# Hybrid HGRN2 and differential-attention block: the adaLN weights arrive in two halves instead of three parts

## The reference, cut to what matters

```python
mod = silu(c) @ w_ada + b_ada                       # 1024 x 3072 weights
shift, scale, gate = split(mod, 3)
h = rms_norm(x, g_pre) * (1 + scale) + shift
proj = h @ w_in                                     # 1024 x 6144
o_a = hgrn2(proj...)  ;  o_b = diff_attention(proj...)
y = (sigmoid(ma) * (o_a @ w_a) + sigmoid(mb) * (o_b @ w_b)) @ w_out
x = x + gate * rms_norm(y, g_post)
```

## Time and profile before

| | |
|---|---|
| median of 3 runs | 928.02 us (925.66 to 929.46) |
| profiled execution | 927.85 us |
| its span | 926.1 us |
| TensorE busy | 855.8 us (92%) |
| VectorE busy | 569.2 us (61%) |
| ScalarE busy | 444.2 us (48%) |
| GpSimd busy | 445.4 us (48%) |
| granted TensorE clock, mean | 0.984 of full |

### The profile page before, as it was taken

How to read it: one execution, slowest core, us unless ns; L and a number is a source line. 1 busy time by engine, 2 the same in 40 slices (tenths; PEclk the granted TensorE clock), 3 DMA queues, 4 the chain that set the end, 5 groups by cost and what they waited for, 6 DMA issues and landing times. The chain is left out here.

```text
span 926.1 us, 12964 instructions
## 1 busy us (share of the span) xinstructions
PE 855.8 (92%) x4825; PEld 673.5 (73%) x4825; DVE 569.2 (61%) x691; ACT 444.2 (48%) x808; POOL 445.4 (48%) x348
## 2 busy tenths in 40 slices
PE   0898799999999999999999999898999999999996
PEld 0786577777777677777777777676788778778885
DVE  3887875688794977776887858545410522892322
ACT  5776322686444865436864436765433710321111
POOL 6042565355455445553554555456778654740000
PEclk9999999999999999999999999999999999999998
DMA  9911341102102110121021021011221732111232
GB/s 330 312 43 50 114 114 46 30 18 69 47 4 66 46 57 13 47 69 31 16 69 47 1 69 46 16 54 46 68 78 37 268 131 80 34 57 46 91 107 75
DMA packets 74481, 68.10 MB, mean 74 GB/s; under 512 B 3700, under 2 KB 65204, under 8 KB 74420
## 3 DMA queue, kind: packets, MB, share of 16 engines
q1 hardware_dynamic: 74304, 67.25, 22.5%
q10 hardware_dynamic: 116, 0.03, 0.0%
HBM read 58.88 MB, written 8.39 MB: 73 GB/s over the span
## 5 line engine op out<-in xcount | busy, mean ns | idle before, releaser
L596 POOL TENSOR_TENSOR w_lo<-w_raw,w_hi 128x512 fp32r<-128x512 f32 x140 | 190.2, 1360 | 279.9 <-ACT w_hi L1145 278.0
L878 PE MATMUL pj<-b_hi,w_hi 128*128 128x512 f32 x616 | 264.6, 430 | 15.0 <-DVE dk L1473 6.5
L880 PE MATMUL pj<-b_hi,w_lo 128*128 128x512 f32 x616 | 243.6, 395 | 0.0
L879 PE MATMUL pj<-b_lo,w_hi 128*128 128x512 f32 x616 | 243.0, 395 | 0.0
L878 PEld LDWEIGHTS pj<-b_hi,w_hi 128*128 128x128 f32 x616 | 117.2, 190 | 54.2 <-issue 9.3
L880 PEld LDWEIGHTS pj<-b_hi,w_lo 128*128 128x128 f32 x616 | 116.9, 190 | 26.3
L879 PEld LDWEIGHTS pj<-b_lo,w_hi 128*128 128x128 f32 x616 | 117.3, 190 | 23.1 <-issue 4.1
L1145 ACT ACTIVATE w_hi<-w_raw 128x512 fp32r<-128x512 f32 x132 | 82.5, 628 | 65.5 <-PE pj L880 58.4
L577 POOL TENSOR_TENSOR w_raw<-w_raw,w_raw 128x512 f32<-128x512 f32 x66 | 93.2, 1412 | 2.9
L1160 ACT ACTIVATE p<-sp,cols 128x1024 f32<-128x1024 f32 (+7 forms) x64 | 46.8, 737 | 0.7
L1298 ACT ACTIVATE y_hi<-y 128x1024 fp32r<-128x1024 f32 x8 | 8.5, 1061 | 76.6 <-DVE y L1669 76.6
(11 more groups left out here) (250 smaller groups left out, 1690.8 us busy)
## 6 DMA issues: line engine op xcount, KB each, us to landing
w_raw<-in_w_in SPq DMA_DIRECT2D x96, 256.0 KB, 4.2
x_in<-in_x SPq DMA_DIRECT2D x8, 512.0 KB, 7.3
ada<-in_w_ada SPq DMA_DIRECT2D x16, 256.0 KB, 7.0
ada<-in_w_ada SPq DMA_DIRECT2D x8, 512.0 KB, 7.1
ada_g<-in_w_ada SPq DMA_DIRECT2D x8, 512.0 KB, 4.6
wo_raw<-in_w_out SPq DMA_DIRECT2D x8, 512.0 KB, 4.2
res<-in_x SPq DMA_DIRECT2D x8, 512.0 KB, 4.3
out_x<-y2n SPq DMA_DIRECT2D x8, 512.0 KB, 2.9
```

The source lines that it names most:

```text
L596: pool.tensor_tensor(w_lo[slot(v)][:, :], raw[:, :], w_hi[slot(v)][:, :].bitcast(F32), ALU.subtract).then_inc(s_wlo, 1)
L878: pe.matmul(bank[:, :], wh, part(b_hi[m], kk), start=(fresh and kk == 0), stop=False, skip_group_check=True)
L879: pe.matmul(bank[:, :], wh, part(b_lo[m], kk), start=False, stop=False, skip_group_check=True)
L880: last = pe.matmul(bank[:, :], wl, part(b_hi[m], kk), start=False, stop=(kk == 3), skip_group_check=True)
```

## The change

The pieces become (0, 4) and (4, 8), each of eight transfers of 512 KB. Tiles 4 to 7 of the second piece lie over tiles 0 to 3 of the first, and SP waits for the first four sums ahead of them. `mod_columns` is done twice instead of three times, with 8 logical products each time: before the first group and after the fourth. On ScalarE `blocks(2, 4)` follows the scaling of x tiles 6 and 7 without a wait. On VectorE the sums of the second piece are interleaved with `block_low(0)` to `block_low(4)`.

```diff
--- before.py
+++ after.py
@@ -118,7 +118,7 @@
 GATEA_AT, MULA_AT = (25, 28), (26, 29)
 GATEA_0, MULA_0 = (30, 33), (31, 34)
 EVICT_AT = {19: (2, 0), 23: (2, 1), 27: (3, 0), 29: (3, 1)}
-PIECES = [(0, 2), (2, 4), (4, 8)]
+PIECES = [(0, 4), (4, 8)]
 
 
 def units(m):
@@ -209,8 +209,7 @@
         b_hi = [block_at(f"b_hi{m}", 4 * m, 2, F32R) for m in range(PROD)]
         b_lo = [block_at(f"b_lo{m}", 4 * m + 2, 2, F32R) for m in range(PROD)]
         b_raw = [block_at(f"b_raw{m}", 4 * m + 2, 2) for m in range(PROD)]
-        ADA_AT = [[8 + kk / 2 for kk in range(KT)], [12 + kk / 2 for kk in range(KT)],
-                  [4 + kk for kk in range(KT)]]
+        ADA_AT = [[8 + kk for kk in range(KT)], [4 + kk for kk in range(KT)]]
         ada = [[block_at(f"ada{p}_{kk}", ADA_AT[p][kk], (b - a) / 4) for kk in range(KT)]
                for p, (a, b) in enumerate(PIECES)]
         acc = block_at("acc", 36, 2)
@@ -482,10 +481,10 @@
                 load_half(half, 0)
             for p, (a, b) in enumerate(PIECES):
                 for kk in range(KT):
-                    if p == 2 and kk == 0:
-                        sp_.wait_ge(s_acc, KT)
+                    if p == 1 and kk == 4:
+                        sp_.wait_ge(s_acc, 4)
                     sp_.dma_start(ada[p][kk][:, :].rearrange("p (z f) -> p z f", z=2),
-                                  w_mod[kk * P:(kk + 1) * P, :, a * P:b * P]).then_inc(s_ada[p % 2][kk // 2], 16)
+                                  w_mod[kk * P:(kk + 1) * P, :, a * P:b * P]).then_inc(s_ada[p][kk // 2], 16)
             for half in range(2):
                 load_half(half, 1)
             for n, t in enumerate((lambda_q1, lambda_k1, lambda_q2, lambda_k2)):
@@ -825,12 +824,10 @@
                     if kk == 0:
                         pe.wait_ge(s_wlo, j + 1)
                     first_product(j, 0, 0, kk)
-                if kk == 0:
-                    mod_columns(1)
-                elif kk < 3:
+                if 0 < kk < 3:
                     for n in range(4):
                         x_block(KT + 4 * (kk - 1) + n)
-            mod_columns(2)
+            mod_columns(1)
             pe.wait_ge(s_xt, 2 * KT)
             for j in range(4):
                 if j == 3:
@@ -1022,7 +1019,6 @@
             blocks(0, 2)
             scale_x(6)
             scale_x(7)
-            act.wait_ge(s_mod, 2)
             blocks(2, 4)
             for n in range(KT, KT + 4):
                 x_out(n)
@@ -1030,7 +1026,7 @@
             for n in range(KT + 4, 2 * KT):
                 x_out(n)
             blocks(5, 8)
-            act.wait_ge(s_mod, 3)
+            act.wait_ge(s_mod, 2)
             blocks(8, 16)
             act.wait_ge(s_lamd, 1)
             act.activation(lam_exp, lam_sum, ACT.Exp).then_inc(s_lame, 1)
@@ -1342,7 +1338,7 @@
                 a, b = PIECES[p]
                 part_acc = acc[:, 2 * P * a:2 * P * b]
                 if kk % 2 == 0:
-                    dve.wait_ge(s_ada[p % 2][kk // 2], 64 if p == 2 else 32)
+                    dve.wait_ge(s_ada[p][kk // 2], 32)
                 if kk == 0:
                     dve.tensor_scalar(part_acc, ada[p][kk][:, :], c_silu[:, 0:1], None, ALU.mult).then_inc(s_acc, 1)
                 else:
@@ -1376,30 +1372,21 @@
             norm(1)
             for kk in range(KT):
                 add_ada(0, kk)
+            mod_piece(0)
             add_ada(1, 0)
+            block_low(0)
             add_ada(1, 1)
-            mod_piece(0)
+            block_low(1)
             add_ada(1, 2)
+            block_low(2)
             add_ada(1, 3)
-            block_low(0)
+            block_low(3)
             add_ada(1, 4)
             add_ada(1, 5)
-            block_low(1)
+            block_low(4)
             add_ada(1, 6)
             add_ada(1, 7)
-            add_ada(2, 0)
             mod_piece(1)
-            add_ada(2, 1)
-            block_low(2)
-            add_ada(2, 2)
-            block_low(3)
-            add_ada(2, 3)
-            add_ada(2, 4)
-            add_ada(2, 5)
-            block_low(4)
-            add_ada(2, 6)
-            add_ada(2, 7)
-            mod_piece(2)
             for e in range(5, 8):
                 block_low(e)
             for kk in range(4):
```

## The result

The changed kernel takes 931.56 us in the median of 13 runs (928.66 to 934.83), the kernel before 926.96 in the median of 13 (925.66 to 930.74). The ratio is 1.0045, interval 1.003 to 1.006: 4.2 us slower (0.0045 x 927), where +4.9 was forecast and 932.9 named. The two medians differ by 4.6 us. By the ratio it lies just inside the 0.5% that the forecast took as its bound, on the side of "no change" (chance 0.42), though the interval excludes 1.000. The profiled execution took 930.91, its span is 929.1.

A forecast was written before the change was run, and what follows sets the result against it. TensorE was taken as busiest, its first product held by a chain of sums, columns and first block. Terms 3.9 + 2.4 - 0.3 - 0.8 - 0.3 = +4.9 us on the median 928.02 gave 932.9, range 929.6 to 935.6.

The forecast's parts named there:

- Part 1: VectorE's first sum, grown from 512 to 1024 columns per tile, ends at 32.50 against 28.59: +3.9 us.
- Part 2: TensorE's first columns take 16 passes instead of 8, mostly at half clock, 3.4 us: +2.4 us.
- Rival (a): Clock stays up through TensorE's first columns, 16 passes at 1.95 us: +3.5 us in all, 931.5; chance 0.26.
- Part 3: From first columns to first product: ScalarE's start follows in 0.43 us instead of 0.70, -0.3 us; the 2.88 behind stay.
- Part 4: Second columns leave TensorE's product stream, -0.8 us; last columns no longer held by the sums, -0.3 us.
- Part 5: ScalarE's 4.03 us wait for the second part goes, without gain; later scaling of x tiles 6 and 7 is hidden.
- rival (d): ScalarE's 4.0 us of waiting sets the stream, so its removal pays back nearly all: 928.9; chance 0.04.
- Part 6: SP waits for four sums instead of eight; modulation weights and `w_raw` loads come earlier; cost and gain 0.
- Rival (b): Half clock lasts longer in TensorE's products, up to +1.2, sum +6.6, 934.6, chance 0.12; if shorter by half, -0.9.
- Rival (c): TensorE's idle times before 82.18 and 112.78 swallow the delay: 928, no change; chance 0.05.

The follow-up runs named there:

- e1_loads: The kernel before with only its transfers in the two halves of the change, sums and columns still in three parts: 928.74 us, ratio 1.0014 to the kernel before.
- e3_warm_after: The changed kernel with 40 identity transposes ahead of the first columns and 28 behind them, to keep the clock up: 929.86 us, ratio 1.0023 to the kernel before.
- second profile: Profile of a repeat of the unaltered changed kernel, on the same chip as its variants: 932.72 us, ratio 1.0046 to the kernel before.
- e4_columns: The kernel before with its first columns computed three times, 24 passes in place of 8: 929.85 us, ratio 1.0026 to the kernel before.

## Why the prediction was right, step by step

- **Part 1 (sums, +3.9)**: measured 10.2 - 6.2 = +4.0. Right. It is read from the traces; no run changes the sums alone. The cover of the transfers was some 1.6 us by e1_loads, 1.4 in the forecast.
- **Part 2 (columns, 3.4 us)**: measured 3.54 in both profiles, near the upper bound. The clock is at half from the start of the columns; e3_warm_after takes it away and gets 1.84. In the first profile it fell only as the columns began, so that the full 3.5 us there was a near thing. Rival (a), the clock stays up, did not occur in a profile of the changed kernel. Two profiles don't exclude it in other executions.
- **Part 3**: from the columns' end (36.47) to ScalarE 0.44, and 39.78 - 36.91 = 2.87 from there, forecast 0.43 and 2.88. First product forecast at 39.3, measured 39.8, of which 0.2 is the later first sum.
- **Part 4**: first product to last columns 55.99 - 39.78 = 16.2, forecast 16.3; the sums ended at 54.2, before TensorE arrived. In the second profile it is 17.1, by the longer half clock.
- **Part 5**: no wait in the stream for the third `b_lo` or for x. ScalarE's 4.03 us of waiting went, 6.13 ahead of the first block took its place, and TensorE gained nothing by the first: rival (d) fails.
- **Part 6**: right. SP issued the four `w_raw` loads from 29.35 instead of 32.83, and GpSimd still waited for TensorE, until 61.28 instead of 57.75.
- **Rival (b)**, a half-clock stretch of differing length, is real but small: twelve products took 4.38 and 5.26 us in two executions of the same kernel. Its sum for a stretch half as long is slightly off: 3.3 us halved saves 0.8, not 0.9.
- **Rival (c)**, swallowing: at 118.39 the profile is 5.6 us late, and e4_columns excludes that all is swallowed. The pause ahead of that place has more in it than the forecast saw: VectorE waits there 3.85 us before and 3.95 after for the gate's weights. But SP issues these transfers when VectorE's `b_lo` is done (106.89 and 112.41), so they move with the work. The sentence that everything behind the last `mod_piece` moves with it was too strong: the forecast put at nothing what VectorE pays beside GpSimd, and this took 1.1 us off the delay at the lambda multiply and put 1.1 on again at 107.48.
- The **size** was 0.7 too large against the ratio (4.2), 0.3 against the medians (4.6), well inside the interval of 2.8 to 5.6. What makes up the 0.7 was not separated; one execution's meetings with GpSimd and half-clock stretches move it by 1.1 to 1.6 us each. That the profiled pair shows 4.1 at 217 us, close to the ratio's 4.2, is chance: it was 5.6 at 118 us, and 2.9 at 542.

Not tried: sums of the first half alone in the changed order (with transfers in three parts), since a sum over four feature blocks needs both parts' data.

## What to carry to other kernels

Where the first use of a result waits for a chain (load, reduce, convert), the size of the first piece sets the start, and merging pieces to have fewer instructions pays the saved time where nothing waits and the added time where all does. Price the first piece alone, from the trace's row of the larger form. When an edit lengthens a pause of TensorE, look at the granted clock of the work right behind it: here 1.7 of the 6.5 us by which the first product is later are the clock's, and with 16 short transposes in the pause the kernel before measured about 0.14% faster, which one of two intervals does not tell from no change. Follow a delay over several marks: here it was 5.2, 4.0, 5.6 and 4.1 us on the way, and any one of them alone would have misled.

## What the runs showed of the hardware

- The clock did not come back during 3.54 us of one-column passes without a gap: in the changed kernel the first products, behind the passes and a pause of 3.30 us, still ran at 1.2 GHz (40.34 and 40.77, 0.43 us apart). With sixteen transposes directly behind full-clock work in the kernel before it stayed at 2.4 GHz over the 1.76 us of pause that followed them and through the products, where without them the products started at 1.2 GHz.
- Executions of one kernel differ by up to some 6 us (925.05 to 930.9 in 35 runs of the kernel before), and they go with the mean granted clock: runs under 926 us had 0.984 to 0.989, those over 930 us 0.980 to 0.981.
- A 64-element multiply on VectorE took 0.21 us alone and 1.31 beside a GpSimd operation on SBUF that had started before it. An operation on 256 elements took 0.43 where GpSimd's started behind it and 1.53 where it started ahead: 1.1 more each time.
